# A sixteen-tile transformer stack on one core: rwkv as a projecting and a state stage, banded attention with a split output projection and input parts loaded from DRAM

## The reference

```python
h = jnp.einsum('btd,de->bte', h_res, w_in[layer])             # first block
...
out = jnp.einsum('bte,ed->btd', mix, w_out[layer])
...
h = rmsnorm(x, norm_g[l])                                     # second block
p = h @ w_in[l]
p_rw = p[..., :RW_COLS]
p_fox = p[..., RW_COLS:RW_COLS + FOX_COLS]
gate = p[..., RW_COLS + FOX_COLS:]
...
def step(state, inp):                                         # rwkv7_branch, per head
    rt, wt, kt, vt, kkt, at = inp
    sa = jnp.einsum('bhvk,bhk->bhv', state, -kkt)
    state = (state * wt[:, :, None, :]
             + sa[..., :, None] * (kkt * at)[..., None, :]
             + vt[..., :, None] * kt[..., None, :])
    yt = jnp.einsum('bhvk,bhk->bhv', state, rt)
    return state, yt
```

## Time and profile before

| what | value |
|---|---|
| time, 3 runs | median 5045.19 us, 5035.6 to 5062.78 |
| profiled execution | 5055.98 us, its span 5054.1 us |
| mean granted clock of TensorE | 0.949 |
| busy | PE 88%, DVE 52%, ACT 26%, POOL 11% |
| stages from the span's start, us | hg 0 to 577, sw to 1333, rw to 2689, fp to 3140, fa to 3742, po to 3958, sh to 4400, rc to 4838, pl to the end |

### The profile page before, as it was taken

The page is one execution under the profiler, slowest core; times in us unless marked ns, Lnnn a source line. Parts: engine busy times, 40 slices in busy tenths (PEclk is TensorE's granted clock), DMA queues, the critical chain, the costliest instruction groups (busy, mean ns, idle before and its releaser), DMA issues. The chain is left out here.

```text
span 5054.1 us, 66269 instructions
## 1 busy us (share of the span) xinstructions
PE 4432.0 (88%) x24491; PEld 3475.6 (69%) x24548; DVE 2603.0 (52%) x5218; ACT 1310.2 (26%) x2645; POOL 558.3 (11%) x537
## 2 busy tenths in 40 slices
PE   8999788888699899889976998799979799699879
PEld 6777566666367667676765887677868577577657
DVE  4444333333166666666664444677753333467733
ACT  3222212222111111111112222566641211222211
POOL 0000011111111111111110111000000011011200
PEclk9999899999799999999987999899989899899979
DMA  2000310111400000000003222611023422422233
GB/s 100 25 19 25 118 44 30 44 44 40 139 20 17 24 20 20 27 14 27 14 12 110 78 83 77 187 34 34 10 86 127 148 102 96 149 89 89 82 123 116
DMA packets 173364, 334.21 MB, mean 66 GB/s; under 512 B 23411, under 2 KB 77172, under 8 KB 173014
## 3 DMA queue, kind: packets, MB, share of 16 engines
q1 hardware_dynamic: 173142, 331.27, 19.4%
HBM read 206.46 MB, written 88.08 MB: 58 GB/s over the span
## 5 line engine op out<-in xcount | busy, mean ns | idle before, releaser
L1161 PE MATMUL rw_pj<-rw_w,rw_hT 128*128 128x512 f32 (+2 forms) x1536 | 498.2, 480 | 19.6 <-ACT rw_hT L153 11.5
L1161 PEld LDWEIGHTS rw_pj<-rw_w,rw_hT 128*128 128x128 f32 x1536 | 273.8, 194 | 220.5 <-issue 183.7
L777 PE MATMUL sw_sc<-sw_wo,sw_mixT 128*128 128x512 f32 x512 | 232.5, 608 | 33.4 <-DVE sw_sm L933 22.6
L235 PE MATMUL fp_pj<-fp_w_high,fp_hT_high 128*128 128x512 f32 (+2 forms) x640 | 222.2, 361 | 31.5 <-DVE fp_w_low L178 19.8
L2274 DVE TENSOR_SCALAR_CACHE_REDUCE fa_sm<-fa_sc 128x512 f32<-128x512 f32 (+2 forms) x320 | 194.4, 610 | 93.2 <-PE fa_sc L2115 83.4
L235 PE MATMUL hg_pj<-hg_w_high,hg_hT_high 128*128 128x512 f32 x512 | 211.0, 412 | 16.0 <-DVE hg_w_low L178 16.0
L235 PE MATMUL rc_pj<-rc_w_high,rc_hT_high 128*128 128x512 f32 (+1 forms) x512 | 192.5, 383 | 33.4 <-DVE rc_w_low L178 33.2
L236 PE MATMUL fp_pj<-fp_w_low,fp_hT_high 128*128 128x512 f32 (+2 forms) x640 | 219.1, 356 | 0.0
L236 PE MATMUL hg_pj<-hg_w_low,hg_hT_high 128*128 128x512 f32 x512 | 205.8, 402 | 0.0
L2129 PE MATMUL fa_tp<-fa_ident,fa_sm 128*128 128x128 f32 x1088 | 175.4, 282 | 31.4 <-DVE fa_pT_low L178 14.7
L777 PEld LDWEIGHTS sw_sc<-sw_wo,sw_mixT 128*128 128x128 f32 x512 | 96.4, 193 | 153.8 <-issue 117.5
(11 more groups left out here) (552 smaller groups left out, 10485.7 us busy)
## 6 DMA issues: line engine op xcount, KB each, us to landing
rc_back<-rc_XB SPq DMA_DIRECT2D x48, 336.0 KB
rw_M<-rw_U SPq DMA_DIRECT2D x16, 728.0 KB, 4.7
hg_xt<-in_x SPq DMA_DIRECT2D x16, 512.0 KB, 3.7
sw_xt<-in_x SPq DMA_DIRECT2D x16, 512.0 KB, 4.9
sw_xres<-in_x SPq DMA_DIRECT2D x16, 512.0 KB, 4.3
x_dram<-sw_y SPq DMA_DIRECT2D x16, 512.0 KB, 3.0
rw_xt<-x_dram SPq DMA_DIRECT2D x16, 512.0 KB, 3.6
fp_xt<-x_dram SPq DMA_DIRECT2D x16, 512.0 KB, 3.7
```

The source lines that it names most:

```text
L235: pe.matmul(out, hT.high[:, kc, :], self.high[:, kc, lo:hi], start=kc == 0, stop=False)
L777: last = pe.matmul(sc[c][:], mixT[:, kc, :], wo[:, kc, c * BANK:(c + 1) * BANK], start=kc == 0, stop=kc == KC - 1)
L1161: last = pe.matmul(pj[pos % 2][:, lo:hi], front.hT[:, kc, :], w[:, kc, a0_ + lo:a0_ + hi], start=kc == 0, stop=kc == KC - 1)
```

## The change

1. hgrn stores both parts of each turned tile of x to DRAM (2 x 512 KB a tile).
2. window_attention loads these parts into one hT instead of turning x; `turn_x`, its casts and the x load go. The output projection's weights and input are split: three F32R matmuls for one F32 matmul, with the low part of the mixed tile made by `low_of_mix` on DVE. The weights' casts come in the first tile (ACT and DVE). xres, hgm, qkv, gate2 and y have one buffer instead of two, and ACT waits for `v_kept` before it refills qkv.
3. rwkv becomes two stages. `rwkv_project` projects with split F32R weights, does the mixing, gates and keys, and stores six 512-column pieces, bonuses and totals of each tile to DRAM, and the parts of the normed x too. `rwkv` loads them and does the state part alone: step i inverts tile i while the state is carried over tile t = i - 1. Copies of X go from DVE to ACT, part of the finish goes from DVE to POOL, and BA, KA, XT and krT have two buffers.
4. fox_project loads the kept parts (two buffers) instead of loading, norming, turning and splitting x.
5. The scratch for dynamic DMA goes from 4096 to 1024.

What stores in hgrn, the pieces of window_attention, and SP's step in `rwkv_project`:

```diff
+                if i is not None:
+                    sp.wait_ge(low_ready, split)
+                    for part, there in zip((hT.high, hT.low), kept):
+                        sp.dma_start(there[rows, :], part[:].rearrange("p k t -> p (k t)").bitcast(F32)).then_inc(kept_there, 16)
                 if t is not None:
...
             def take_x(i):
+                need(act, kept_there, 32 * i)
...
+            def load_parts(rows):
+                for part, there in zip((hT.high, hT.low), kept):
+                    sp.dma_start(part[:].rearrange("p k t -> p (k t)").bitcast(F32), there[rows, :]).then_inc(hT_here, 16)
...
-            def turn_x(i, hi, pi):
-                pe.wait_ge(x_here[pi], 16 * (hi + 1))
-                need(pe, taken[1], i)
-                need(pe, low_ready, 2 * i)
-                for g in range(2):
-                    for c in range(4):
-                        last = pe.transpose(turned_banks[g][:, c * P:(c + 1) * P], xt[pi][:, (4 * g + c) * P:(4 * g + c + 1) * P], ident[:])
-                    last.then_inc(x_turned, 1)
...
+                    cols = slice(c * BANK, (c + 1) * BANK)
                     for kc in range(4 * half, 4 * half + 4):
-                        last = pe.matmul(sc[c][:], mixT[:, kc, :], wo[:, kc, c * BANK:(c + 1) * BANK], start=kc == 0, stop=kc == KC - 1)
+                        pe.matmul(sc[c][:], mixT.high[:, kc, :], wo.high[:, kc, cols], start=kc == 0, stop=False)
+                        pe.matmul(sc[c][:], mixT.high[:, kc, :], wo.low[:, kc, cols], start=False, stop=False)
+                        last = pe.matmul(sc[c][:], mixT.low[:, kc, :], wo.high[:, kc, cols], start=False, stop=kc == KC - 1)
                     if half == 1:
...
-                    turn_x(i, hi, pi)
                     project(i, 0, 0, SW).then_inc(chunk_ready, 1)
...
+            def low_of_mix(t, n):
+                dve.wait_ge((hg_high, a_high)[n], t + 1)
+                mixT.take_low(dve, lambda ap: ap[:, 4 * n:4 * n + 4, :], heads((th, tp[1])[n][:], 4)).then_inc((hgT_ready, aT_ready)[n], 1)
...
+                if i is not None:
+                    if not (isinstance(i, int) and i == TILES - 1):
+                        front.load(sp, i + 1)
+                    sp.wait_ge(front.low_ready, split)
+                    for part, there in zip((front.parts.high, front.parts.low), kept):
+                        sp.dma_start(there[rows_i, :], part[:].rearrange("p k t -> p (k t)").bitcast(F32)).then_inc(kept_there, 16)
+                    shift(i, hi, pi, t is None)
...
+                    sp.dma_start(packed[rows_t, AT["kk"]:AT["kk"] + RW], kk[:]).then_inc(kb_stored, 16)
+                    sp.dma_start(packed[rows_t, AT["b"]:AT["b"] + RW], b[:]).then_inc(kb_stored, 16)
+                    for n, at in enumerate(("r", "k", "v")):
+                        sp.dma_start(packed[rows_t, AT[at]:AT[at] + RW], M[pt][:, n * RW:(n + 1) * RW]).then_inc(m_stored[pt], 16)
...
+                if i is not None:
+                    sp.wait_ge(taken[4], i + 1)
+                    sp.dma_start(packed[rows_i, AT["gate"]:AT["gate"] + RW], gate2[:]).then_inc(gate_stored, 16)
```

PE in the state stage, the read-out and the step:

```diff
+                for p in range(PAIRS):
+                    cols = slice(p * P, (p + 1) * P)
+                    pe.matmul(B[INC_BANK][:, cols], given_of(pt, "k")[:, cols], V[:, cols], start=p == 0, stop=False)
+                pe.wait_ge(XT_ready, PER_TILE * (t + 1))
+                pe.wait_ge(Z_ready, t + 1)
                 for h in range(RW_HEADS):
                     cols = slice(h * RW_DIM, (h + 1) * RW_DIM)
-                    last = pe.matmul(B[1][:, cols], XT[:, h, :], Z[:, cols], start=True, stop=True)
+                    last = pe.matmul(B[Z_BANK][:, cols], XT[pt][:, h, :], Z[:, cols], start=True, stop=True)
                 last.then_inc(SA_done, 1)
...
+                follows = pr and not (isinstance(i, int) and i == TILES - 1)
                 if pr:
-                    front.turn(pe, i, (taken[4], taken[2]))
-                    project(i, 0).then_inc(chunk_ready, 1)
...
-                if m:
+                    if not m:
+                        for two in range(2):
+                            turn_two(0, 0, 0, two, None)
                     for n in range(2):
                         for r in range(2):
-                            multiply(t, n, r)
+                            multiply(i, pi, n, r)
+                    spread(i)
+                if m:
+                    if pr:
+                        pe.wait_ge(masked, 8 * i + 8)
+                    solve(t, pt)
+                    read_out(t, pt)
                 if pr:
-                    project(i, 4).then_inc(chunk_ready, 1)
-                if m:
-                    spread(t)
-                    solve(t, pt)
+                    if not m:
+                        pe.wait_ge(masked, 8)
                     for g in range(2):
-                        turn_first(t, g)
+                        turn_first(i, pi, g)
                     for l in range(FIRST, LEVELS):
                         for g in range(2):
-                            level(t, l, g, 0)
+                            level(i, pi, l, g, 0)
                         for g in range(2):
-                            level(t, l, g, 1)
-                    read_out(t, pt)
+                            level(i, pi, l, g, 1)
+                        if follows and l < FIRST + 2:
+                            turn_two(i + 1, hi + pi, 1 - pi, l - FIRST, t)
```

fox_project:

```diff
-        front = Normed(s, x, norm_g, ident, tf[2:4], split=True)
+        front = Kept(s, *kept)
...
-                    front.turn(pe, i)
                     for c in range(2):
-                        project(i, c)
+                        project(i, hi, pi, c)
```

More of the change, by code:

```diff
@@ L1112, in _ @@
+            assert len(small) + 1 == CONSTS
             for dst, src in small:
                 sp.dma_start(dst, src).then_inc(consts_in, 16)
[L1114 to L1124 removed]
@@ L1326, in _, with take_two @@
             act.wait_ge(set_up, 1)
-            front.square(act, 0)
-            def take(i, pi, c, t=None, ht=None, pt=None):
-                pos = ORDER.index(c)
-                act.wait_ge(chunk_ready, 5 * i + pos + 1)
-                lo, hi = COLS[c]
-                if c == 4:
-                    need(act, taken[4], i)
-                    act.activation(tanh, pj[0][:], ACT.Tanh, scale=0.5).then_inc(tanh_ready, 1)
-                    return
-                if c == 0:
-                    if t is not None:
-                        act.wait_ge(shifted[pt], shift_count(ht, pt))
-                act.copy(U[pi][:, lo:hi], pj[pos % 2][:, 0:hi - lo]).then_inc(taken[c], 1)
+            def take_two(n, pn, two):
+                for one in range(2):
+                    act.wait_ge(turned, 4 * n + 2 * two + one + 1)
+                    bank = B[TURNED[2 * two + one][1]]
+                    if two == 0:
+                        act.copy(krT[pn][:, :, one, :], heads(bank[:], PAIRS)).then_inc(krT_ready, 1)
+                    else:
+                        act.copy((bT, kT)[one][:], heads(bank[:], PAIRS)).then_inc(bkT_ready, 1)
@@ L1368, in step @@
-                if pr:
-                    take(i, pi, 2)
-                if m:
-                    for n in range(2):
-                        act.wait_ge(turned4, 4 * t + n + 1)
-                        act.copy(krT[:, :, n, :], heads(B[n][:], PAIRS)).then_inc(krT_ready, 1)
-                if pr:
-                    if not (isinstance(i, int) and i == TILES - 1):
-                        front.square(act, i + 1)
-                    take(i, pi, 4)
+                follows = pr and not (isinstance(i, int) and i == TILES - 1)
@@ L1378, in step @@
+                if pr and not m:
+                    for two in range(2):
+                        take_two(0, 0, two)
                 if m:
                     act.wait_ge(Z_done, t + 1)
-                    act.activation(Z[:], B[4][:], ACT.Copy, scale=-1.0).then_inc(Z_ready, 1)
+                    act.activation(Z[:], B[Z_BANK][:], ACT.Copy, scale=-1.0).then_inc(Z_ready, 1)
+                    act.wait_ge(SA_done, t + 1)
+                    act.copy(SA[:], B[Z_BANK][:]).then_inc(SA_ready, 1)
+                    act.wait_ge(y_done, t + 1)
+                    act.copy(y[:], B[Y_BANK][:]).then_inc(y_ready, 1)
@@ L1606, with fox_project @@
 FX_DIM = 64
-def fox_project(nc, x, norm_g, w_in, q_g, k_g, b_f, masks, keys, values, cum3, queries, gates):
+def fox_project(nc, kept, w_in, q_g, k_g, b_f, masks, keys, values, cum3, queries, gates):
     with ExitStack() as ctx:
```

995 lines of the change are left out of this document (568 added, 427 removed).

## The result

The changed kernel takes 5109.69 us (median of 4 runs, 5106.91 to 5111.44) against 5045.62 for the kernel before in the same comparison (5035.6 to 5062.78). The ratio is 1.0123, 95% interval 1.0095 to 1.0151: 1.2% slower, where I had forecast no change (5041) and slower with a chance of 0.45. The time is inside the range (4930 to 5140), which was drawn to hold rivals 1 and 3 too.

What follows compares the result with a forecast made beforehand. PE's own instruction list was taken to bound sw, rw and fp. rwkv +83 and the rest -87 (1 - 58 - 30) gave 5056 - 4 = 5052, less 11: 5041 us, no change; range 4930 to 5140.

Steps and rivals of the forecast that it cites:

- rival 1: State stage: clock stays at half until the levels; period 57.1 us a tile, +75, 5116 us; chance 0.20.
- rival 3: State stage: DVE's masks and compaction slower beside POOL's four operations; 5 us a tile, +75, 5116 us; chance 0.10.
- state stage: New second rwkv stage: 60 for the first tile, 15 x 52.1, 34 for the last, 876 us in all.
- 1439: Both rwkv stages together, 563 + 876 us against 1356 before; missing it by more than 40 would show the forecast wrong.
- Start: Work from the profiled execution's 5056 us, then take 11 off at the end because the runs' median was 5045.19.
- hgrn, fox_project: hgrn's extra stores cost +1 us in all; fox_project loses transposes and cast wait, 1.82 us a tile, -30 in all.
- window_attention: Banded attention loses turn, low-part wait and some F32 time: -4.2 us a tile, first gate 8 later, -58 in all.
- rwkv_project: New projecting stage, split F32R chunks: 31.3 us a tile on PE, 563 us in all, bounds 530 and 610.
- T: State stage: last correction of the tile before, with which multiply starts; spread was to start at T + 10.0.
- the -80: rwkv tiles: gain of cheaper projections, (78.1 - 31.3 - 52.1) x 15, said to be lost to uncovered waits and slow clock.
- Rival 2: State stage: clock comes back inside spread; 45.9 us a tile, -93, 4948 us; chance 0.22.

Runs made afterwards that it cites:

- experiment 1: The kernel before with hgrn and window_attention of the changed kernel, rwkv and fox_project as they were: 5007.18 us against 5051.51, ratio 0.9918.
- experiment 4: The changed kernel with POOL's four gain and rest operations waiting until the split of the compacted blocks is done: 5044.44 us against 5051.51, ratio 0.999.
- experiment 6: The changed kernel with three idle dense F32 matmuls (128x512) between spread and solve: 5039.15 us against 5049.34 for the kernel before, ratio 0.9982.
- experiment 3: The changed kernel with six idle F32 matmuls (128x512) in PE's wait between multiply and spread: 4952.16 us against 5051.51, ratio 0.9812.
- experiment 8: The changed kernel with POOL's gain and rest operations behind the blocks' split and three idle 128x512 F32 matmuls before spread: 4894.11 us against 5049.34, ratio 0.9694.
- experiment 7: The changed kernel with 48 idle F32R matmuls of 128 columns, spread's form, in the wait before spread: 5103.33 us against 5049.34, ratio 1.012.

## Why the prediction was wrong

The mechanism was the forecast's: PE's uncovered wait, the clock that falls in it, spread and solve at half. The step that failed is the sum of the state stage, which priced two of its terms too low, and the sign hung on them. rwkv's two stages took 1482, 43 more than the forecast's 1439; the forecast had named a miss of more than 40 as the sign that it is wrong.

- **Start.** I worked from 5056 and took 11 off, the distance of the profiled execution to the median before. After the change the profiled execution took 5108.83 and the median is 5109.69. So 11 of the 69 us of error were the choice to carry that distance over.
- **hgrn, fox_project.** hgrn's stage is 572.4 long as before. fox_project: -30 forecast, 468.7 - 439.0 = 29.7 measured. Right.
- **window_attention.** -58 forecast, -50 in the traces, -44 in experiment 1. The period fell by 3.5, not 4.2: the low part of the mixed tile holds PE for 1.40 us (below, from the changed kernel) where the copy held it for 0.68. First tile's gate 6.4 later, as forecast (8).

```profile
939.37 0.50 PE L797 MATMUL sw_sc<-sw_wo_high,sw_mixT_high 128*128 128x512 f32 x1 [1.40 <-DVE sw_mixT_low L178]
```

- **rwkv_project.** 563 forecast, 549.3: an error of 14 us the other way, by luck, that hid a part of the state stage's 57. The wait for the cast was as in the earlier trace rows; its tiles take 30.6 (first and last use of one operation, 1348.7 to 1807.6), the figure before I added 0.7.
- **State stage, the step that failed.** 876 forecast, 933.1. Per tile: spread at T + 11.3, not 10.0; spread 6.9 and solve 10.2, as forecast; read-out 8.9, not 7.9; turn_first 1.8, not 1.0; levels with the transposes 16.0, not 16.2. Sum 55.1 against 52.1, 45 us in the stage; its first tile and its end took 12 more. The 1.3 is what the forecast put at nothing, POOL's four operations beside the compaction (a part of rival 3, shown by experiment 4): 8.5 us from the first mask to spread, not 7.0. The masks, which rival 3 had named as its sign, were not longer (2.47); it was the copy and the compaction that were. The 1.8 is a part of rival 1: the clock was back for only part of the read-out in 11 tiles, and not before the levels in 4, where rival 1 held in full and read-out and turn_first took 13.1 together instead of 10.7.
- **A reading that was off.** The 78.1 us a tile of the earlier trace rows average in the first step, which has no state part and took 46.6; the steady tile of the kernel before is 80.3 (1434.99 to 2559.8, 14 periods). It stood in the explanation of the -80 alone; the sum used the stage's 1356.
- **What no sum showed.** The stages from fa on took 1903 and 1896, 6 us apart with the same instructions. The spread of such sums over my traces is of that size.

The rivals: 1 gave 5116 and 3 gave 5116, each for 5 us a tile, and of these came 1.8 and 1.3; that the truth (5110) lies near both figures is not their merit. I gave the two 0.30 together and put the forecast where neither happened at all; both could only cost. Rival 2, the clock coming back inside spread, is refuted by every tile of the changed kernel. The rule of the Trainium skill that I set against the rows ("TensorE: Matmul & The Clock Gate", Part 1, activity releases the throttle) is not borne out here where PE was merely busy: spread and solve were busy 4.00 of 4 us at 0.50 for 17.1 us, and three dense matmuls between them brought the clock back (experiment 6).

The right price of the moved cover can be written from the runs: the clock cost 158 us (experiment 3) and POOL's place 65 (experiment 4), and without them the same change is worth -155 (experiment 8: 4894 against 5049). What is left of the wait itself is still in that figure, filled with idle matmuls.

## What to carry to other kernels

Before a chunk of work is taken out from between two dependent steps, price the wait that it covered twice: the wait itself, and what runs behind it at half clock, until the clock is back. A busy PE is not a sign of full clock: read the granted clock of the stretch behind the wait, in every tile and not in one, since neighbouring tiles differed here. A few matmuls of 512 columns, even idle ones, in the wait or behind it were worth many times their time. And read a small operation's duration with what the other engines do beside it: the row of before for the compaction was already stretched.

## What the runs showed of the hardware

- Spread and solve take 9.4 us at 2.4 GHz and 17.1 at 1.2 GHz. Gapless, they stayed at a granted clock of 0.50 for all of it in the 15 steady tiles of the changed kernel. 48 matmuls of spread's form ahead of them held the full clock in 5 of 15 tiles and not in 10 (experiment 7).
- Six F32 matmuls of 128x512: behind waits of 1.5 to 1.6 us the clock did not fall (7 tiles); behind 2.70 us it fell as they started and was back after 3.4 us (7 tiles, experiment 3). Three of them between two sparse blocks brought it back within 2.5 us of their start, in the first tile within 4.7 (experiment 6).
- The levels, matmuls of 128 and 64 columns each with its own weights, ran at 1.00 (38 records in 4 us).
- DVE beside POOL: four operations of 32x128 took 1.41 us alone, 2.44 where POOL's products lay beside their first half in the kernel before, and 4.14 beside POOL throughout; a copy of 128x128 between SBUF tensors took 0.23 alone and 1.13 beside POOL. Masks that read from PSUM took 2.47 to 2.48 both ways. The Trainium skill, "GPSIMD Engine Reference", section 1, says that GpSimd shares its SBUF interfaces with VectorE and that they contend when a VectorE instruction has two SBUF inputs or runs in a 2-port mode; the trace agrees for the four operations, which have two such inputs (1.41 and 4.14). In which mode the copy ran, no run shows.
